# An attention output projection in three fp32r products of high and low parts, with the first expert weights loaded after it

## What is computed

```python
mix = o @ w_out[l]                                   # 512x1024 @ 1024x1024
x = layer_norm(DN_ALPHA * x + mix, ln1_g[l], ln1_b[l])
ffn = moe_ffn(x, router_w[l], ...)                   # 64 experts, 8 per token, and a shared one
x = layer_norm(DN_ALPHA * x + ffn, ln2_g[l], ln2_b[l])
```

## Time and profile before

| | us |
|---|---|
| Median of 3 runs | 2259.81 (2257.76 to 2261.32) |
| The profiled execution: its time | 2263.92 |
| The profiled execution: its span | 2261.7 |
| Busy in the span: PE, DVE, ACT, POOL | 2111.1, 1626.6, 1378.4, 661.8 |
| Mean granted TensorE clock | 0.966 |

### The profile page before, as it was taken

One profiled execution on the slowest core, in us unless ns is written; L12 is line 12 of the kernel. 1 busy time (PEld: TensorE's weight loads), 2 busy tenths in 40 slices (PEclk: granted clock), 3 DMA queues, 4 the chain that ended last, 5 costly groups with the idle time before them and its releaser, 6 DMA issues. The chain is left out here.

```text
span 2261.7 us, 31680 instructions
## 1 busy us (share of the span) xinstructions
PE 2111.1 (93%) x10838; PEld 1603.5 (71%) x10838; DVE 1626.6 (72%) x2281; ACT 1378.4 (61%) x1754; POOL 661.8 (29%) x358
## 2 busy tenths in 40 slices
PE   6999999799999999997779999997999999999957
PEld 4778865577777777775366888566777777777743
DVE  2484432799999999996445834347999999999946
ACT  3533741388888888885034347215888888888831
POOL 0010200044444444443311020001444444444323
PEclk9999999899999999998889999998999999999979
DMA  5312142399999999998931230434999999999978
GB/s 195 93 48 77 83 166 108 111 354 369 381 382 371 372 374 384 380 377 326 376 96 56 66 140 1 175 131 172 366 377 379 381 364 378 375 373 374 370 305 331
DMA packets 135898, 595.87 MB, mean 263 GB/s; under 512 B 29380, under 2 KB 55492, under 8 KB 79736
## 3 DMA queue, kind: packets, MB, share of 16 engines
q1 hardware_dynamic: 102264, 527.43, 61.9%
q0 software_dynamic: 33536, 67.18, 8.9%
HBM read 577.83 MB, written 69.76 MB: 286 GB/s over the span
## 5 line engine op out<-in xcount | busy, mean ns | idle before, releaser
L1348 PE MATMUL ps_up<-w_hi,rowsT_hi 128*112 128x512 f32 x1024 | 424.0, 414 | 15.0 <-DVE rowsT_lo L1442 14.7
L1350 PE MATMUL ps_up<-w_hi,rowsT_lo 128*112 128x512 f32 x1024 | 406.3, 397 | 0.0
L1296 POOL DMA_INDIRECT y_rows<-y,index x128 | 210.2, 1642 | 611.3 <-ACT y L1517 595.5
L1288 POOL DMA_INDIRECT rows<-x_rows,index x128 | 329.6, 2575 | 149.4 <-issue 90.3
L1430 DVE TENSOR_TENSOR w_lo<-w,w_hi 128x2048 fp32r<-128x2048 f32 x128 | 292.5, 2287 | 50.8 <-ACT w_hi L1482 50.7
L1430 DVE TENSOR_TENSOR w_next_lo<-w_next,w_hi 128x2048 fp32r<-128x2048 f32 x128 | 292.7, 2287 | 29.0 <-ACT w_hi L1482 29.0
L1482 ACT CAST w_hi<-w 128x2048 fp32r<-128x2048 f32 x128 | 245.1, 1916 | 51.8 <-PE ps_up L1350 32.6
L1482 ACT CAST w_hi<-w_next 128x2048 fp32r<-128x2048 f32 x128 | 245.2, 1915 | 26.5 <-PE ps_up L1350 23.6
L1348 PEld LDWEIGHTS ps_up<-w_hi,rowsT_hi 128*112 128x112 f32 x1024 | 183.0, 179 | 59.9 <-issue 15.3
L1350 PEld LDWEIGHTS ps_up<-w_hi,rowsT_lo 128*112 128x112 f32 x1024 | 179.9, 176 | 59.9
L1373 PE MATMUL ps_y<-w_hi,hiddenT_hi 128*112 128x512 f32 x512 | 211.2, 412 | 5.4 <-DVE hiddenT_lo L1449 3.9
(11 more groups left out here) (244 smaller groups left out, 4312.1 us busy)
## 6 DMA issues: line engine op xcount, KB each, us to landing
w_next<-exp_w SPq DMA_DIRECT2D x204, 1024.0 KB, 10.0
w<-exp_w SPq DMA_DIRECT2D x136, 1024.0 KB, 16.4
w_first<-exp_w SPq DMA_DIRECT2D x34, 1024.0 KB, 11.9
w_last<-exp_w SPq DMA_DIRECT2D x32, 1024.0 KB
wbuf<-w_in SPq DMA_DIRECT2D x16, 1024.0 KB, 5.6
got<-y_rows SPq DMA_DIRECT2D x8, 2048.0 KB, 23.0
got<-y_rows SPq DMA_DIRECT2D x16, 1024.0 KB, 26.0
w_out_sb<-w_out SPq DMA_DIRECT2D x2, 4096.0 KB, 19.5
```

What stands on the lines that cost most here:

```text
L1288: pool.indirect_dma_start(rows[0:CAP, x.slot, :], None, d["x1_rows"], bass.IndirectOffsetOnAxis(ap=index[0:CAP, x.step, 0:1], axis=0), bou ...
L1296: pool.indirect_dma_start(d["y_rows"], bass.IndirectOffsetOnAxis(ap=index[0:CAP, x.step, 1:2], axis=0), y[0:CAP, x.slot % 2, :], None, bou ...
L1348: pe.matmul(ps_up[b][0:CAP], hi, w_hi, start=(k == 0), stop=False)
L1350: mm = pe.matmul(ps_up[b][0:CAP], lo, w_hi, start=False, stop=(k == KD - 1))
```

## The change

w_out is split, in four quarters of two pieces each, into a high part (ScalarE, `upper(q)`) and a low part (VectorE, `lower(q)`), and so is each transposed tile of o (`copy_o` gives the high part, `lower_o` the low one). mix(t) makes three fp32r products for each fp32 one, with the piece k as the outer loop. The low part of w_out is written over w_out itself; its high part lies in `w13`, the memory of the up weights of experts 0 and 1, and the low part of o in `w2_first`. So these experts' first weights are loaded only once the mix is over: on SP's queue `_load_up(0)` comes after mixed(4) and ahead of the last x1 store, the others behind it. VectorE's table columns (L1053 to L1056) now come behind the splits.

```diff
-        oT = T("oT", [P, 2, KD, P])
+        oT_hi, oT_lo = T("oT_hi", [P, 2, KD, P], F32R), sb["oT_lo"]
+        w_out, w_out_hi, w_out_lo = sb["w_out"], sb["w_out_hi"], sb["w_out_lo"]
@@ sync
-                _load_down(sp, d, sb, l, 0, S["ahead_in"])
-                for e in range(2):
-                    _load_up(sp, d, sb, l, e, S["ahead_in"])
                 for t in range(NT):
+                    if t == NT - 1:
+                        sp.wait_ge(S["oT_made"], NT)
+                        sp.wait_ge(S["mixed"], NT)
+                        _load_up(sp, d, sb, l, 0, S["ahead_in"])
                     sp.wait_ge(S["x1_ready"], t + 1)
                     sp.dma_start(d["x1_rows"][t * P:(t + 1) * P, :], x_sb[:, t, :]).then_inc(S["x1_out"], 16)
-                sp.wait_ge(S["oT_made"], NT)
-                sp.wait_ge(S["mixed"], NT)
+                _load_down(sp, d, sb, l, 0, S["ahead_in"])
+                _load_up(sp, d, sb, l, 1, S["ahead_in"])
                 _load_up(sp, d, sb, l, 2, S["ahead_in"])
@@ tensor
                 def turn_o(t):
                     if t:
                         pe.wait_ge(S["oT_out"], t)
+                        pe.wait_ge(S["oT_low"], t)
...
                 def mix(t):
-                    pe.wait_ge(S["oT_out"], t + 1)
+                    pe.wait_ge(S["oT_low"], t + 1)
                     if t:
                         pe.wait_ge(S["row_sum"], t)
-                    for c in range(2):
-                        for k in range(KD):
-                            mm = pe.matmul(ps_mix[:, c * 512:(c + 1) * 512], oT[:, t % 2, k, :],
-                                           sb["w_out"][:, k, c * 512:(c + 1) * 512], start=(k == 0), stop=(k == KD - 1))
+                    for k in range(KD):
+                        if t == 0 and k % 2 == 0:
+                            pe.wait_ge(S["out_lo"], k // 2 + 1)
+                        hi, lo = oT_hi[:, t % 2, k, :], oT_lo[:, t % 2, k, :]
+                        for c in range(2):
+                            out, cols = ps_mix[:, c * 512:(c + 1) * 512], slice(c * 512, (c + 1) * 512)
+                            pe.matmul(out, hi, w_out_hi[:, k, cols], start=(k == 0), stop=False)
+                            pe.matmul(out, hi, w_out_lo[:, k, cols], start=False, stop=False)
+                            mm = pe.matmul(out, lo, w_out_hi[:, k, cols], start=False, stop=(k == KD - 1))
@@ scalar
-                    act.copy(oT[:, t % 2].rearrange("p k c -> p (k c)"), flat_a).then_inc(S["oT_out"], 1)
+                    act.copy(oT_hi[:, t % 2].rearrange("p k c -> p (k c)"), flat_a).then_inc(S["oT_out"], 1)
+
+                def upper(q):
+                    act.copy(w_out_hi[:, 2 * q:2 * q + 2, :], w_out[:, 2 * q:2 * q + 2, :]).then_inc(S["out_hi"], 1)
...
+                upper(0)
                 copy_o(0)
+                upper(1)
                 copy_o(1)
+                upper(2)
+                upper(3)
@@ vector
+                def lower_o(t):
+                    dve.wait_ge(S["oT_out"], t + 1)
+                    dve.tensor_tensor(oT_lo[:, t % 2].rearrange("p k c -> p (k c)"), flat_a,
+                                      oT_hi[:, t % 2].rearrange("p k c -> p (k c)").bitcast(F32), ALU.subtract
+                                      ).then_inc(S["oT_low"], 1)
+
+                def lower(q):
+                    dve.wait_ge(S["out_hi"], q + 1)
+                    dve.tensor_tensor(w_out_lo[:, 2 * q:2 * q + 2, :], w_out[:, 2 * q:2 * q + 2, :],
+                                      w_out_hi[:, 2 * q:2 * q + 2, :].bitcast(F32), ALU.subtract).then_inc(S["out_lo"], 1)
+
+                lower(0)
+                lower_o(0)
+                lower(1)
+                lower_o(1)
+                lower(2)
+                lower(3)
...
                     _norm_centre(dve, S, r[:, t % 2, :], st, gain, x_sb[:, t, :], t)
+                    if t + 2 < NT:
+                        lower_o(t + 2)
                     _norm_variance(dve, S, st, t)
@@ trunk
+                    sb["w_out_lo"] = view("w_out_lo", [P, KD, D], F32R, behind)
+                    sb["w_out_hi"] = w13[1][:].rearrange("p s a k f -> p (s a k f)").rearrange("p (k c) -> p k c", k=KD)
+                    sb["oT_lo"] = w2[1][:].rearrange("p j (k c) -> p (j k) c", c=P).rearrange("p (s k) c -> p s k c", s=2)
```

More of the change, by code:

```diff
@@ L847, in _mix_and_route @@
         S = _named(ctx, nc, NORM_SEMS + " norm_in small_in shared_in oT_made oT_out mixed mix_read x1_ready x1_out x1T_made x1T_out "
-                            "logits_made exps up_made silu_out gated rows_cleared scaled hot_ready picked_made index_ready "
+                            "logits_made exps up_made silu_out gated out_hi out_lo oT_low rows_cleared scaled hot_ready picked_made index_ready "
                             "rows0_in rows1_in rows2_in ahead_in mask_ready pos_made route_step tables square_in tokens")
         T = lambda name, shape, dt=F32: ctx.enter_context(nc.sbuf_tensor(name, shape, dt))
-        oT = T("oT", [P, 2, KD, P])
+        oT_hi, oT_lo = T("oT_hi", [P, 2, KD, P], F32R), sb["oT_lo"]
+        w_out, w_out_hi, w_out_lo = sb["w_out"], sb["w_out_hi"], sb["w_out_lo"]
         r = T("r", [P, 2, D])
@@ L984, in _ @@
                 pe.wait_ge(S["oT_out"], NT)
+                pe.wait_ge(S["oT_low"], NT)
                 router(NT - 2)
```

## The result

The changed kernel has a median of 2247.64 us over 5 runs (2246.88 to 2249.93), the kernel before 2260.2 us over 5 (2257.76 to 2263.9): 12.6 us less. The ratio is 0.9945, with a 95% interval of 0.9933 to 0.9958, so clear of no change. The profiled execution has a span of 2245.9 us (before 2261.7). A second measurement, beside three experiments on one chip, gave 2247.94 us and 0.9947 (0.9933 to 0.996). The kernel before was measured twice more, beside the experiments: 2259.73 us over 18 runs, one of which took 3047.94 us at a granted clock of 0.649 and is left out of every ratio, and 2260.25 over 9.

A forecast was written before the change was run, and what follows sets the result against it. TensorE was taken to bound the projection stage from tile 1 on. Products -16.9 us and tile 0 +0.6, with the other work and loads hidden, sum to -16.3: from 2259.8 to 2243.5 us, range 2240 to 2251.

The forecast's parts named there:

- What bounds the stage: Output projection (mix): from tile 1 on bound by TensorE alone, one tile taking 13.81 us without a gap.
- Part 1, the products: Tiles 1 to 3, both layers: 48 fp32r products at 0.229 us, 10.99 us a tile instead of 13.81; -16.9 us.
- Rival (e): Mix products stream with no cost of their own: 0.214 us each, a tile 10.3 us, 2237.7 us; chance 2%.
- Part 2, the chain: Tile 0's start: operands split first, first product at +7.25 instead of +4.03, then 48 products, partly at half clock.
- Part 2, the balance of tile 0: Two new tile 0 ends, 38.7 us, against the measured 38.07: +0.6 us for both layers (-0.8 to +2.0).
- Part 3: lower_o(2) and lower_o(3), 1.22 us each, sit between centring and variance of tiles 0 and 1 on VectorE, at no cost.
- Part 4, the loads: 11.5 MB of expert weights, loaded after the mix, land at 402.1; 11.6 us of slack hide them.
- The span: The profiled execution's whole span: from 2261.7 to 2245.4 us.
- (a): Block start: GpSimd's memset holds up lower(0), 1.57 us per layer, 3.1 in all, 2246.6 us; chance 7%.
- (b): The start in bursts keeps the clock at 1.2 GHz through tile 0; gain gone, +0.5, 2260.3 us; chance 7%.
- (c): Late weights become the block's last wait; at half DMA rate 15.4 us late per layer, +14.5, 2274.3 us; chance 5%.
- (d): More gain in the mix: fp32r steps at 0.227 us and little half clock, -18.5, about 2241 us; chance 4%.

The follow-up runs named there:

- the order by itself: The changed kernel with o's copy and low part before w_out's, and tile 0's high-by-low products last: 2244.04 us, ratio 0.9934.
- the fillers by themselves: The changed kernel with five unread fp32 products of 256 columns on TensorE between turn_o(0) and turn_o(1): 2244.43 us, ratio 0.9924.

## Why the prediction was right or wrong

The forecast of 2243.5 was 4.1 us low; the range, 2240 to 2251, holds the 2247.6. Step by step:

- **What bounds the stage**: right. Two, three and two-halved products gave tiles of 9.2, 12.8 and 15.4 us between the same events.
- **Part 1, the products**: the mechanism is right, the size 1.1 us too large. 48 products took 11.17 us from the first to the next operation, 0.231 each after 0.08 at the start, the experts' step of the earlier trace rows and not the mean with that of the earlier trace rows: 15.8 us, not 16.9. The row with the weights as the wide operand was the nearer one, and I had said so. Rival (e) is out.
- **Part 2, the chain**: right. First product at +7.12 (I said +7.25); lower_o(0) 1.22 us as worked out from two halves; last part of w_out at +14.84 (+15.0); no stall of tile 0 in the trace. One reason in it was wrong: I expected the start at half clock because of the long pause, and in the first layer of this execution the clock had fallen before that pause began.
- **Part 2, the balance of tile 0**: this is the term that was mis-sized. I set two new ends against the two measured ones and got +0.6 us. The four starts of the old kind give t0 of 18.6 on average, the six of the new kind (both layers of the changed kernel twice, and of the kernel with the loads after the tables, 20.29 and 20.43) 19.9. So tile 0 costs 1.2 us per layer, **2.5 in all**. Most of the difference, 1.4 us, is that I took the 20.07 of one execution for the kernel's own, when its half clock was one draw; the new tile 0 ended 0.3 us per layer later than my middle. With it: -15.8 + 2.5 = -13.3, against -12.6 and -12.3 measured. The last microsecond is within the scatter. That the forecast came within 4.1 us is no luck of opposite errors: both terms erred towards too large a gain.
- **Part 3**: right. lower_o(2) and lower_o(3) show no wait behind them, and t2 and t3 shrink like t1. The cast at L1053 took 0.74 us when the memset was over.
- **Part 4, the loads**: right in what mattered, the slack (11.8 us, 11.6 forecast): landed at 402.5 (402.1), vector work over at 414.3 (413.7). That the landing fits to half a microsecond is luck. I counted all loads from 375.0, while the first two were issued from 370.16 on, and I left out the store of x1 between them and the time from the last byte (the rate is 49 GB/s in 401 to 402) to SP's release.
- **The span**, 2245.9 where I said 2245.4, agrees too well: the profiled execution of before was 3.7 us above its runs' median and that of the changed kernel at its median, so that excess went into the difference.
- **Rivals**: (a) is out: lower(0) started at +1.95 and took 2.29 us beside the memset, as the Trainium skill (SBUF — State Buffer, Who interferes with whom) has it. (b) is true in part: the clock was 0.50 until about 321 and 0.94 in 321 to 323, 9 products at half clock but never the tile. (c) did not occur; the loads moved behind the routing tables show that its price is as I reckoned or higher. (d) did not occur: the step was 0.231 and not 0.227, and the half clock cost tile 0 1.84 us in the first layer (13.01 us against 11.17).

## What to carry to other kernels

Where a product of fp32 takes two halves of 0.43 us, three fp32r products of 0.231 save a fifth, but only for tiles whose parts are ready: the first tile pays for the splits. Start the chain that frees the next transfer or transpose first, take the products that need the fewest parts first, and keep TensorE busy while it would wait: together, with the table's columns moved, this gave 8.1 us here; the order by itself gave 3.9 and the fillers by themselves 3.5, which the times don't set clear of no gain. Before a first tile's time is used as a term, look at it in more than one layer or execution: its clock is a draw.

## What the runs showed of the hardware

- The granted clock at the same point differs between executions: in one kernel 0.50 and 1.00 in 319 to 321, with t0 of 20.41 and 19.23; in two kernels that differ only in their loads 0.61 and 1.00 in 311 to 313, with t0 of 20.07 and 17.29.
- A cast of 128x256 to bf16 took 4.07 us beside GpSimd's memset and 0.74 alone, while a subtraction of two 128x2048 operands beside the same memset took its usual 2.29. This agrees with the Trainium skill's page SBUF — State Buffer (Who interferes with whom), which lets the first kind be locked out and not the second.
- While weight loads shared the DMA with gathers of rows (0.71 MB), both together moved 315 to 366 GB/s, where the weights alone move 424, and the gathers took 12.2 us to land and not 3.5.
